# Four high products, then four low products, in a weight chunk of a two-block float32 kernel

## The reference

```python
h = rms_norm(x, pre_mix_norm); p = h @ w_in            # then four mixers side by side
x = x + rms_norm(concat(y_a, y_b, y_c, y_d) @ w_out, post_mix_norm)
h = rms_norm(x, pre_ffn_norm)
gate, val = split(causal_dwconv(h @ ffn_up))
x = x + rms_norm((gelu(gate) * val) @ ffn_down, post_ffn_norm)
x = x + 0.5 * (silu(h1 @ ffn1_gate) * (h1 @ ffn1_up)) @ ffn1_down      # second layer
proj = rms_norm(x, mix_norm) @ w_in_2                  # dilated and differential attention
x = x + (sigmoid(g_dil) * (o_dil @ w_dil) + sigmoid(g_diff) * (o_diff @ w_diff)) @ w_out_2
x = x + 0.5 * (silu(h2 @ ffn2_gate) * (h2 @ ffn2_up)) @ ffn2_down
```

## Time and profile before

| what | value |
|---|---|
| median of 3 runs | 3356.85 us (3355.34 to 3358.34) |
| profiled execution | 3355.8 us, of it 3354.0 us span of the core |
| granted TensorE clock over the span | 1.000 |
| TensorE busy | 3336.8 us (99%) |
| VectorE, ScalarE, GpSimd busy | 67%, 52%, 16% |
| DMA | 616.21 MB, mean 184 GB/s |

### The profile page before, as it was taken

How to read it: one execution, slowest core, us unless ns; L and a number is a source line. 1 busy time by engine, 2 the same in 40 slices (tenths; PEclk the granted TensorE clock), 3 DMA queues, 4 the chain that set the end, 5 groups by cost and what they waited for, 6 DMA issues and landing times.

```text
span 3354.0 us, 59341 instructions
## 1 busy us (share of the span) xinstructions
PE 3336.8 (99%) x19746; PEld 2930.5 (87%) x19746; DVE 2238.2 (67%) x2874; ACT 1745.4 (52%) x2588; POOL 533.8 (16%) x502
## 2 busy tenths in 40 slices
PE   9999999999999999999999999999999999999999
PEld 8888888888888888888888888888888888888888
DVE  7878587777744565655555699766687655655544
ACT  5455565555544554544444555554565554544443
POOL 0215111111100011111100066511100111111000
PEclk9999999999999999999999999999999999999999
DMA  6535555555566555555566655545556555555665
GB/s 214 163 114 157 183 171 190 189 189 191 187 193 189 179 180 194 188 188 192 188 190 191 215 175 175 190 156 160 172 192 199 192 188 192 189 188 191 186 194 174
DMA packets 176036, 616.21 MB, mean 184 GB/s; under 512 B 20912, under 2 KB 21584, under 8 KB 175568
## 3 DMA queue, kind: packets, MB, share of 16 engines
q1 hardware_dynamic: 175520, 609.84, 57.0%
q10 hardware_dynamic: 432, 5.24, 0.4%
HBM read 610.81 MB, written 4.19 MB: 183 GB/s over the span
## 4 chain that ended last, share of the span: by engine, by line
PE 94%; DVE 3%; issue 1%; ACT 1%; DMA 1%; POOL 0%; DVEq 0%; SPq 0%; ACTq 0%; POOLq 0%
PE acc L462 59%; PE acc L465 30%; DVE weights_low L312 1%; PE ps_wide L391 1%; PE acc L477 1%; ACT weights_high L305 0%; PE ps_narrow L2551 0%; PE ps_wide L2527 0%; PE acc L480 0%; DVE halves_memory L567 0%; PE ps_scale L2932 0%; DMA weights_raw<-in_w_in 0%; DMA weights_raw<-in_w_diff_branch 0%; DVE halves_memory L3010 0%; ACT arena L801 0%
## 5 line engine op out<-in xcount | busy, mean ns | idle before, releaser
L462 PE MATMUL acc<-moving_halves,weights_high 128*128 128x512 f32 x6304 | 1971.2, 394 | 1.9 <-DVE x_T L2820 1.9
L312 DVE TENSOR_TENSOR weights_low<-weights_raw,weights_high 128x1024 fp32r<-128x1024 f32 (+1 forms) x1172 | 1431.2, 1235 | 716.7 <-ACT weights_high L305 715.7
L305 ACT ACTIVATE weights_high<-weights_raw 128x1024 fp32r<-128x1024 f32 (+1 forms) x1172 | 1207.8, 1032 | 768.7 <-PE acc L465 741.9
L465 PEld LDWEIGHTS acc<-moving_halves,weights_low 128*128 128x128 f32 x6304 | 1183.8, 188 | 262.0
L465 PE MATMUL acc<-moving_halves,weights_low 128*128 128x256 f32 x6304 | 1244.8, 279 | 0.0
L462 PEld LDWEIGHTS acc<-moving_halves,weights_high 128*128 128x128 f32 x6304 | 957.5, 188 | 12.0 <-issue 9.8
L462 PE MATMUL acc<-gated_halves,weights_high 128*128 128x512 f32 x2024 | 627.9, 392 | 0.0
L561 ACT ACTIVATE cross_products<-acc 128x256 f32<-128x256 f32 x503 | 193.0, 384 | 666.3 <-PE acc L465 666.2
L465 PEld LDWEIGHTS acc<-gated_halves,weights_low 128*128 128x128 f32 x2024 | 380.1, 188 | 83.5
L584 POOL TENSOR_TENSOR stage_scratch<-unscaled,token_scale 128x256 f32<-128x256 f32 x260 | 215.0, 827 | 1279.9 <-DVE unscaled L567 802.4
L465 PE MATMUL acc<-gated_halves,weights_low 128*128 128x256 f32 x2024 | 399.3, 279 | 0.0
(11 more groups left out here) (384 smaller groups left out, 2008.7 us busy)
## 6 DMA issues: line engine op xcount, KB each, us to landing
weights_raw<-in_w_in SPq DMA_DIRECT2D x268, 512.0 KB, 3.9
weights_raw<-in_ffn_up SPq DMA_DIRECT2D x176, 512.0 KB, 4.5
weights_raw<-in_ffn_w_gate SPq DMA_DIRECT2D x176, 512.0 KB, 4.2
weights_raw<-in_ffn_w_up SPq DMA_DIRECT2D x176, 512.0 KB, 4.8
weights_raw<-in_ffn_w_down SPq DMA_DIRECT2D x160, 512.0 KB, 3.9
weights_raw<-in_ffn_down SPq DMA_DIRECT2D x80, 512.0 KB, 3.8
weights_raw<-in_w_out SPq DMA_DIRECT2D x64, 512.0 KB, 3.9
weights_raw<-in_ffn_w_down SPq DMA_DIRECT2D x32, 256.0 KB, 2.7
```

The lines of the kernel that those rows point to most:

```text
L305: core.nc.scalar.activation(core.high[:, slot, k0:nk, :].rearrange("p a b -> p (a b)"), core.raw[:, slot, k0 * P:nk * P], ACT.Copy).then_i ...
L312: core.nc.vector.tensor_tensor(core.low[:, slot, k0:nk, :].rearrange("p a b -> p (a b)"), core.raw[:, slot, k0 * P:nk * P], core.high[:, s ...
L462: core.nc.tensor.matmul(acc[:, t % 2, :, :], core.high[:, u % SLOTS, k, :], parts[:, prod.first[t] + k0 + k, :, :], start=(k0 + k == 0), s ...
L465: core.last = core.nc.tensor.matmul(acc[:, t % 2, 0, :], core.low[:, u % SLOTS, k, :], parts[:, prod.first[t] + k0 + k, 0, :], start=False ...
```

## The change

Within a chunk the k are taken in fours: four high products, then four low products. `multiply_pair` gets a parameter `n`, 2 by default, and is called with 4 from the two ordinary loops. A joined tile keeps its order (two calls of two k), and the woven body keeps its pairs. Chunks have eight or four k, so no group is short. The number and the kinds of instructions stay as they are, and the waits stay in front of the same high products; what follows a high product or a low product in the queue is other than before.

```diff
@@ multiply_after_full
-            for pair in range(0, nk, 2):
-                multiply_pair(core, prod, acc, t, u, pair, k0, operand.on(pe))
+            for four in range(0, nk, 4):
+                multiply_pair(core, prod, acc, t, u, four, k0, operand.on(pe), 4)
             core.last.then_inc(core.slots_free, 1)
@@ multiply
-        for pair in range(0, nk, 2):
-            (multiply_joined if joined else multiply_pair)(core, prod, acc, t, u, pair, k0, before)
+        for four in range(0, nk, 4):
+            if joined:
+                multiply_joined(core, prod, acc, t, u, four, k0, before)
+                multiply_joined(core, prod, acc, t, u, four + 2, k0, before)
+            else:
+                multiply_pair(core, prod, acc, t, u, four, k0, before, 4)
         core.last.then_inc(core.slots_free, 1)
@@
-def multiply_pair(core, prod, acc, t, u, pair, k0, before):
+def multiply_pair(core, prod, acc, t, u, pair, k0, before, n=2):
...
-    ks = range(pair, min(pair + 2, nk))
+    ks = range(pair, min(pair + n, nk))
     for k in ks:
         if before is not None:
             before(t, prod.first[t] + k0 + k)
```

## The result

| | before | after |
|---|---|---|
| median of 22 runs each | 3357.04 us (3354.41 to 3358.44) | 3362.04 us (3360.45 to 3366.78) |
| ratio | 1 | 1.0016, interval 1.0010 to 1.0022 |
| profiled execution | 3355.8 us, span 3354.0 | 3361.4 us, span 3359.5 |

The loss is 5.0 us, inside the 0.2% that was called no change, but the interval shows that it is real. It has the other sign than the forecast (0 to -4 us), and 3362.0 us lies 1 us above the forecast's own range of 3350 to 3361. The page has the same engines at the same work; line 466 is the high product now, line 469 the low one.

The account below looks back on a forecast made before the run. TensorE's start-to-start distances bound the kernel. From the profiled 3355.8 us, less 2.2 us for the groups plus 0.5 us for waits gave 3354, or 3355 as median; range 3330 to 3380, the forecast's own 3350 to 3361.

Parts of the forecast that it names:

- What bounds the kernel: TensorE, busy 99% at full clock: time is the number of products times the distance between their starts; weights always ready.
- the price of the trade: Per group of four k, two switches between kinds become one more repetition of each: 0 to -2 ns, 0 to -4 us.
- The low term: One more repetition of low products in each group of four k, at 1.4 ns less (115.6 against 117).
- The high term: One more repetition of high products in each group of four k: nothing, as no row has a run of them.
- the prediction's own sign: The forecast is wrong if the distance of the groups, 1.38 us in clean stretches, is off by more than 3 ns.
- The present order already visits both the quick and the dear distances in turn and averages over them: Reason for taking the point for a group of four k at the present 1380 ns.
- The quick lock: Rival: runs of four low products hold 113.3 ns each, -17 ns a group; every second group gives 3337 us; chance 0.32.
- The slow lock: Rival: low runs at 117.9 ns, last two highs at 235, +22 ns a group; every second group gives 3380 us; chance 0.24.
- The bounds of a group: Four high and four low products take 1360 to 1419 ns, -20 to +39 from now, -45 to +88 us in all.
- The waits: In first tiles, low products now stand behind waits for later activation parts: counted 0, bound +1.2 us; 0.5 in the sum.
- The rule of the Trainium skill: A matmul costs columns over 2.4 GHz plus 2.5 ns: 1300 ns for a group in either order, so no change.
- Slow lock's reason: The next weight load, 188 ns in the profile beside a 117 ns low product, runs late; four lows leave less catching up.

Follow-up runs that it names:

- e8: Kernel before with its pairs, but the low product reads both activation parts and is 512 columns wide too; a single run of 4350.1 us.
- e14: Kernel before reordered in seven products: pairs, then groups 1, 4, 3 in first tiles, then 3, 3, 2 and 2, 3, 3 in turn; 3344.50 us, 0.9966.
- e15: As e14, but loop chunks of eight are 3, 3 and a pair with halved high products, chunks of four two halved pairs; 3334.66 us, 0.9936 of before.
- e12: Kernel before with groups 1, 4, 3 first in each body, otherwise 3, 3 and a pair with halved high products, mostly halved pairs for four k; 1.0131.
- e2: Kernel before with fours only in tiles with a wait before each high product and the body after a plain float32 product; pairs elsewhere; 1.0003.
- e7: Kernel before with groups 3, 3, 2 (3, 1 in a chunk of four), high products of a chunk of eight's last two k halved; 1.0110.

## Why the prediction was wrong

- **What bounds the kernel** was right: the distance of the starts on TensorE. The granted clock stayed at 1.00 and the idle time in front of high products at 2.6 to 3.9 us, and the fourteen versions that changed only the order of products or halved some (the change itself and all with a time but e8) moved the time by -0.6% to +1.7%.
- **The failed step is the price of the trade:** "One more repetition of low products at 1.4 ns less, and nothing for the high ones, of which no row has a run: 0 to -2 ns in a group". The low term was right: -2.0 ns, the mean low product went from 116.0 to 115.5. (The rows give 117.5 for the former, which the prediction wrote as 117, and both are too high; its 115.6 for the latter was near.) The high term was set to nothing for want of a row, without a bound in the sum, and it is +5.3 ns. Together that is +3.3 ns, 7.5 us over 2246 groups in place of 0 to -4. By the prediction's own sign, off by more than 3 ns, the forecast failed. Behind that stands a false form: a price for each transition. By the table a group's price depends on the state in which it begins, and the fours reach state B, where their first two highs take 233 and 236, which pairs in the loop never do.
- **"The present order already visits both the quick and the dear distances in turn and averages over them"** was right, also for the fours, and it is why the change moved so little. Every second low run is quick, 453 ns, and the others take 471. That the dear and the quick then cancel to 3.3 ns was not foreseen by any term of the sum; that the time came so near is in part luck. Neither rival came in its size, but a part of each did. The quick lock's low runs of 453 ns come in every second group. The slow lock's dear highs do too, 930 ns for four (+14), but as the first two of the four and not the last two, and the other groups give back 3 ns. Both states can be held in other orders (e14 and e15 hold the quick one, e12 the slow one, +1.3%).
- **The bounds of a group,** 1360 to 1419 ns, held in ffn_up's loop for all kernels with 512 and 256 columns; the best order found has 1367, the worst 1413.
- **The waits** at 0 to +1.2 us: e2, at 1.0003 (0.9994 to 1.0012), fits but can't tell 1 us. The idle time in front of the high products did not grow (3.1 us, 3.3 before).
- **The rule of the Trainium skill** ("TensorE: Matmul & The Clock Gate", section "Back-to-back issue gap"), columns over 2.4 GHz plus 2.5 ns, knows no state, and the section calls it the gap of an isolated matmul. The trace disagrees with it for a stream with a weight load each: a long run of 512 columns has 228.9 ns here against its 215.8.
- **Slow lock's reason,** a late weight load under short products, was not shown. Against it, 132 products of 256 columns with a load for each ran in a row at 113.3 ns in the joined tiles.

## What to carry to other kernels

When the busiest engine is TensorE with nothing to wait for, compare start-to-start distances over a whole period of the loop. If equal instructions have unequal distances, suspect a state, and test it with the same loop entered in two ways, as e7 and e15 do here. An order that avoids the dear state gains without a change in the work. Prices that were read in one pattern don't carry to another: set no term to nothing because no row shows it, but bound it, or run the new pattern once. Enter the quick state deliberately after each interruption, and choose groups that keep it, here groups of three. They keep a dear state as faithfully (e7, e12), so check in the trace which one it is.

## What the runs showed of the hardware

- The start-to-start distance of float32r matmuls with a weight load each, at granted clock 1.00, is not a function of the instruction and its neighbour. In the joined tiles 256 columns take 113.3, 117.8 on the mean, or 120 ns (w_out) for as long as the run lasts. 512 columns in a long run take 225.8, 229.2 and 231.7 in turn (e8), but 226.7 each in e8's w_out.
- The state survives chunks and tiles: e15 holds the quick one through ffn_up's loop and e7 the dear one. After other matmuls the first high product takes 315 to 423 ns in eight of ten cases (kernel before), and the state after it can be another: e7 is quick in the first chunk of ffn_up and dear from the next interruption on.
- The operand of w_out settles at 120 ns (119.7 over the thirty matmuls of the earlier trace rows) where the others settle at 113.3 or 117.8, in the kernel before, the changed one and e8. Whether its place in memory is the reason was not tried.
- What the state is in the hardware stays open. The runs show its transitions, not its cause.
